# The first weight block of a transformer layer's last projection is split two products before the MLP ends, and the projection's PSUM banks swap parity

## The reference

```python
x = x + mix @ w_out                                   # mix: long convolution and attention
h = _rmsnorm(x, mlp_norm_w) @ w_mlp1
x = x + jnp.square(jax.nn.relu(h)) @ w_mlp2
gate = jax.nn.sigmoid(x @ w_ple_gate)
x = x + gate * _rmsnorm(p_l @ w_ple_proj, ple_norm_w)
```

## Time and profile before

| | |
|---|---|
| median of three runs | 1794.86 us (1792.33, 1794.86, 1794.9) |
| the profiled execution | 1794.4 us, its span 1792.6 us |
| TensorE matmul busy | 1745.6 us, 97% of the span |
| TensorE weight load busy | 1583.3 us, 88% |
| VectorE busy | 1332.4 us, 74% |
| ScalarE busy | 728.3 us, 41% |
| GpSimd busy | 408.2 us, 23% |
| mean granted TensorE clock | 0.993 of full speed |

### The profile page before, as it was taken

The page is one execution under the profiler, slowest core; times in us unless marked ns, Lnnn a source line. Parts: engine busy times, 40 slices in busy tenths (PEclk is TensorE's granted clock), DMA queues, the critical chain, the costliest instruction groups (busy, mean ns, idle before and its releaser), DMA issues.

```text
span 1792.6 us, 26437 instructions
## 1 busy us (share of the span) xinstructions
PE 1745.6 (97%) x10563; PEld 1583.3 (88%) x10563; DVE 1332.4 (74%) x1671; ACT 728.3 (41%) x1149; POOL 408.2 (23%) x256
## 2 busy tenths in 40 slices
PE   8999999999999999999999999999899999999999
PEld 5566788888899987888999999999899999998887
DVE  4695376887999988579765555557999898996634
ACT  6112311246777778146333333334233333333511
POOL 0000000003222220001222222124848373840000
PEclk9999999999999999999999999999999999999999
DMA  9223145132110013423232222328241413102121
GB/s 361 87 77 129 65 172 178 62 147 79 51 42 21 16 60 117 146 104 131 76 130 99 99 94 100 105 77 320 83 175 31 170 42 141 42 1 77 36 93 60
DMA packets 59058, 183.65 MB, mean 102 GB/s; under 512 B 6901, under 2 KB 7669, under 8 KB 58424
## 3 DMA queue, kind: packets, MB, share of 16 engines
q1 hardware_dynamic: 58936, 181.96, 28.6%
HBM read 138.58 MB, written 43.35 MB: 101 GB/s over the span
## 4 chain that ended last, share of the span: by engine, by line
PE 81%; DVE 11%; ACT 3%; issue 2%; DMA 2%; SPq 1%; POOL 0%; DVEq 0%; ACTq 0%; POOLq 0%
PE ps L3247 40%; PE ps L2724 21%; PE ps L3107 3%; PE ps L3135 3%; PE ps L3119 2%; PE ps L2783 2%; PE ps L2810 2%; PE ps L2822 2%; DVE K L1655 1%; PE ps L3016 1%; DVE ptl L2299 1%; PE ps L2771 1%; DVE gmax L2252 1%; DMA wst<-wb 1%; DVE cv L1655 1%
## 5 line engine op out<-in xcount | busy, mean ns | idle before, releaser
L3247 PE MATMUL ps<-rV,ringh 128*128 128x320 f32 x1248 | 235.8, 311 | 9.0 <-issue 7.0
L3247 PE MATMUL ps<-rU,ringh 128*128 128x320 f32 x1088 | 204.3, 310 | 3.3 <-issue 2.1
L3247 PEld LDWEIGHTS ps<-rV,ringh 128*128 128x128 f32 x1248 | 197.1, 189 | 10.7 <-issue 8.2
L2724 PE MATMUL ps<-XL,wh 128*128 128x512 f32 x708 | 179.0, 361 | 0.0
L3247 PEld LDWEIGHTS ps<-rU,ringh 128*128 128x128 f32 x1088 | 170.5, 188 | 4.8 <-issue 3.4
L2480 DVE TENSOR_TENSOR fH<-ps,fH 128x640 f32<-128x640 f32 x112 | 90.7, 822 | 112.1 <-PE ps L3247 112.0
L2724 PE MATMUL ps<-XH,wh 128*128 128x512 f32 (+1 forms) x612 | 164.6, 378 | 6.5 <-DVE wl L1632 2.8
L2724 PE MATMUL ps<-XH,wl 128*128 128x512 f32 (+1 forms) x612 | 154.4, 361 | 0.0
L3247 PE MATMUL ps<-rV,ringl 128*128 128x320 f32 x624 | 142.7, 310 | 0.0
L2724 PEld LDWEIGHTS ps<-XH,wh 128*128 128x128 f32 x612 | 105.0, 191 | 40.0 <-issue 18.7
L3247 PE MATMUL ps<-rH,ringh 128*128 128x320 f32 x736 | 137.9, 309 | 1.3 <-DVE rH L2425 1.3
(11 more groups left out here) (408 smaller groups left out, 3893.3 us busy)
## 6 DMA issues: line engine op xcount, KB each, us to landing
hd<-fH SPq DMA_DIRECT2D x64, 320.0 KB, 2.3
wst<-wb SPq DMA_DIRECT2D x34, 512.0 KB, 3.4
wst<-wm SPq DMA_DIRECT2D x30, 512.0 KB, 3.7
fU<-hd SPq DMA_DIRECT2D x32, 320.0 KB, 4.0
fH<-hd SPq DMA_DIRECT2D x24, 320.0 KB, 3.9
wraw<-wm SPq DMA_DIRECT2D x14, 512.0 KB, 3.7
w2b<-wm SPq DMA_DIRECT2D x12, 512.0 KB, 7.2
xraw<-xT SPq DMA_DIRECT2D x8, 640.0 KB, 10.2
```

Source lines behind the costliest of these rows:

```text
L2724: ins = mm(acc(jslot)[:, o:o + n], sub(a[slot], s), b[:, o:o + n], start=(first and k == 0 and a is wh and b is xh), stop=(last and k == l ...
L3247: ins = mm(out[:, c, :], a[:, w], two(b(xs[kk]))[:, c, :], start=kk == 0 and a is h and b is hi_of, stop=kk == 3 and a is l)
```

## The change

The split of B_PLE moves up on both engines: ScalarE's waits for product 221 in place of 222, and VectorE's stands ahead of the sum of product 223, with a wait for product 221. The sixteen jobs of the projection and the gate take the accumulator of their own parity in place of the other one, and the projection's first two jobs wait for the sums of products 222 and 223, by name. The split of B_PLE+1 stays where it was.

```diff
@@ ScalarE
-            split(B_PLE, (mm_done, product_done(222)))
+            split(B_PLE, (mm_done, product_done(221)))
             split(B_PLE + 1, (mm_done, product_done(223)))
 ...
-                fn((dsq if m else dss)[:, :], acc(J_PLE + m + 1), ACT.Square).then_inc(pp_sq, 1)
+                fn((dsq if m else dss)[:, :], acc(J_PLE + m), ACT.Square).then_inc(pp_sq, 1)
                 act.wait_ge(acc_free, J_PLE - NPROD + m)
-                fn(pp[m], acc(J_PLE + m + 1), ACT.Copy).then_inc(acc_free, 1)
+                fn(pp[m], acc(J_PLE + m), ACT.Copy).then_inc(acc_free, 1)
 ...
-                    fn(dsq[:, :], acc(j + 1), ACT.Sigmoid).then_inc(acc_free, 1)
+                    fn(dsq[:, :], acc(j), ACT.Sigmoid).then_inc(acc_free, 1)
@@ VectorE
+            dve.wait_ge(mm_done, product_done(221))
+            split(B_PLE, B_PLE % 2)
             output_sum(111)
-            dve.wait_ge(mm_done, product_done(222))
-            split(B_PLE, B_PLE % 2)
             dve.wait_ge(mm_done, product_done(223))
             split(B_PLE + 1, (B_PLE + 1) % 2)
@@ TensorE
                 if m % 4 == 0:
                     weights_ready(B_PLE + m // 4)
                 if m < 2:
-                    pe.wait_ge(ps_read, PS_READ + 112 + 110 + 2 * m)
-                linear(J_PLE + m, J_PLE + m + 1, (B_PLE + m // 4) % 2, (2 * (m % 4), 2 * (m % 4) + 1),
+                    pe.wait_ge(ps_read, PS_READ + 112 + 111 + m)
+                linear(J_PLE + m, J_PLE + m, (B_PLE + m // 4) % 2, (2 * (m % 4), 2 * (m % 4) + 1),
                        x2[6:8], [(h_lo, 1), (h_lo, 2)])
 ...
-                linear(J_GATE + m, J_GATE + m + 1, (B_GATE + m) % 2, range(KD), x2)
+                linear(J_GATE + m, J_GATE + m, (B_GATE + m) % 2, range(KD), x2)
```

More of the change, by code:

```diff
@@ L1471, in _ @@
                         act.wait_ge(mm_done, j + 1 + c)
-                        fn(dsq[:, o:o + n], acc(j + 1)[:, o:o + n], ACT.Sigmoid).then_inc(acc_free, 1)
+                        fn(dsq[:, o:o + n], acc(j)[:, o:o + n], ACT.Sigmoid).then_inc(acc_free, 1)
                 if m < 6:
@@ L3285, in _ @@
                 weights_ready(B_GATE + m)
-                linear(J_GATE + m, J_GATE + m + 1, (B_GATE + m) % 2, range(KD), x2,
+                linear(J_GATE + m, J_GATE + m, (B_GATE + m) % 2, range(KD), x2,
                        [(n_lo, KD + 28 + 112 + 1 + k) for k in range(KD)] if m == 0 else (),
@@ L3290, in _ @@
                 weights_ready(B_GATE + m)
-                linear(J_GATE + m, J_GATE + m + 1, (B_GATE + m) % 2, range(KD), x2)
+                linear(J_GATE + m, J_GATE + m, (B_GATE + m) % 2, range(KD), x2)
             weights_ready(B_GATE + 6)
-            linear(J_GATE + 6, J_GATE + 7, B_GATE % 2, range(KD), x2)
+            linear(J_GATE + 6, J_GATE + 6, B_GATE % 2, range(KD), x2)
             weights_ready(B_GATE + 7)
@@ L3297, in _ @@
             for o, n in TOKENS:
-                ins = passes(acc(J_GATE + 8)[:, o:o + n],
+                ins = passes(acc(J_GATE + 7)[:, o:o + n],
                              [((sub(wh[last], k), sub(wl[last], k)), (x2[k][0][:, o:o + n], x2[k][1][:, o:o + n]))
```

## The result

| | before | changed |
|---|---|---|
| median of ten runs | 1792.74 us | 1788.36 us |
| lowest to highest | 1790.85 to 1794.9 | 1787.3 to 1791.08 |
| the profiled execution (its span) | 1794.4 (1792.6) | 1789.74 (1788.0) |

The ratio is 0.9979, 95% interval 0.9971 to 0.9987: about 3.8 us (2.3 to 5.2). So the changed kernel is faster, though the interval doesn't say that it is by over 0.2%; the two medians alone differ by 4.4 us. The forecast was a gain of 3.65 us, 0.203%. But its time, 1791.2, stands 2.8 us above the measured median, and its range of 1789.6 to 1793.4 misses it. The gain was right within what the runs can tell, and the base it was taken from was not: the median of before's first three runs, 1794.86, was 2.1 us above that of ten.

What follows compares the result with a forecast made beforehand. TensorE was taken as the bound (busy 97% of the span). Pause 2.05 plus clock fall 1.60 gave 3.65 us, other edits 0: 1794.86 - 3.65 = 1791.2 us, range 1789.6 to 1793.4.

Steps and rivals of the forecast that it cites:

- The base: Before's time from which the gain was subtracted: 1794.86 us, the median of three runs.
- one more fall in luck: Low end of the range: one further clock fall of 1.6 us missing from the whole run, giving 1789.6 us.
- The pause: TensorE's idle time between the MLP's last product and the last (PLE) projection, all removed: 2.05 us.
- the seam's unknown: Remainder where the projection's first matmul follows the last product without a wait: within 0.3 us either side, taken as 0.
- The clock fall: Projection's first nine matmuls, slow behind the pause, run at full clock: 3.37 us becomes 1.77, saving 1.60.
- half the gain: Rival: the pause goes but no clock fall is saved, or the side sums get one; 1792.8 us, chance 0.25.
- The edits at nothing: ScalarE's earlier split, VectorE's reordered split, the swapped banks, and the second block with its load: each priced at 0.
- The slack of the split: VectorE's early split of B_PLE ends at about 1639.0, before the sum of product 223 at 1640.49: 1.5 us.
- nothing waits at the side sums: Answers the slower rival: late projection additions make TensorE wait at the side sums, with a fall; 1796.5 us, chance 0.04.
- rival of an unfinished split: VectorE's split not over when product 223 ends, so part of the pause stays; 1791.9 to 1794.2 us, chance 0.08.

Runs made afterwards that it cites:

- f3: The kernel before, unchanged, measured against itself: 0.9999 of before, runs from 1790.8 to 1795.23 us.
- e1: The changed kernel with ScalarE's copy of the first weight block waiting for product 222 again: 0.9977 of before, median 1789.06 us.
- e3: The kernel before with only the bank parity and its waits changed, both splits left where they were: 1.0002 of before.
- e2: The kernel before with both splits of the first block early, old bank parity, job 0 waiting for the sum of product 223: 0.9992 of before, median 1790.54 us.
- f1: The kernel before with TensorE's pause ahead of the last projection filled by twelve matmuls whose result is thrown away: 0.9999 of before.
- g1: The kernel before with the pause filled by twelve thrown away matmuls, the same kernel as f1 once more: 0.9999 of before.
- g3: The changed kernel with the side sums and the broadcast one step later: 0.9988 of before, median 1790.94 us.
- h1: The kernel before with the pause filled by thrown away matmuls and the side sums' one-column matmuls in two halves: 0.9989 of before.
- h2: The kernel before with three runs of twenty one-column matmuls in halves (near 220 and 343 us, and the side sums): 0.9999 of before, runs 1791.87 to 1793.22 us.

## Why the prediction was right or wrong

**The base: the step that failed.** "1794.86 - 3.65 = 1791.2" took the median of three as the kernel's time, where ten runs gave 1792.74. Over 126 runs before's mean is 1792.8 with a standard deviation of 1.2, and the profiled execution (clock 0.993) was of the quarter with the lowest clock, with falls near 222 and 345. Both come and go: 5 and 6 of the 14 profiles with undivided sums there have them. With the better base of 1792.74 the same sum gives 1789.1, 0.7 above the median measured, and the same range 1787.5 to 1791.3, which holds it.

**The range: too narrow on the low side.** It allowed "one more fall in luck". The prediction had the evidence for more in hand: three runs 2.6 us apart, and a fall at 219.53 named as uncertain. It used them for the seam's fall and the side sums', but not for the base.

**The pause and the seam: right, the remainder a little off.** All 2.05 us of idle time went. The first matmul came 2.21 us earlier behind the last product's last group (2.50 to 0.29), so the seam's unknown, bounded by 0.3 us and taken as 0, was 0.16 in the change's favour.

**The clock fall: right in kind and in size.** The term was 1.60, and the nine matmuls now take 1.62 us less; behind them nothing more was gained (33.46 against 33.47 us up to the side sums). The prediction also held it possible that some runs of before escaped this fall, and put 0.25 on half the gain. In the five profiles with a pause of 2 us or more at the seam it was never missing; what differs from run to run is other falls. The Trainium skill (TensorE: Matmul & The Clock Gate, "What's actually happening") says that slow matmuls differ in number from run to run of one kernel, and the traces agree (before's first profile has seven falls, f3's six); the step from that to this place was mine. The time lost to the clock fell by 1.5 us, close to a whole fall.

**The edits at nothing: right.** ScalarE's Copy (e1), the parity by itself (e3), the load and the second block cost nothing. The slack of the split was 1.56 us, forecast 1.5. The additions ended at 1669.31 + 1.49 = 1670.8, 3.86 ahead of the side sums at 1674.66, where before had 3.87: they moved up with TensorE. That job 0 under the old parity "could not have used the earlier split" was too strong: e2 used it for 1.09 of the 2.05 us.

**The rivals.** No pause was left and nothing waits at the side sums, so those two fall. Two figures of the rival of an unfinished split didn't follow from its own working. A block landing at 1637 leaves no pause: the Copy and the split would end near 1639.3, ahead of product 223, and e1, whose Copy started as late as before's, had none. And its upper end of 1794.2 is 0.7 above the 0.7 us of pause and a fall of 1.6 that it names (1793.5). The rival of half the gain named the side sums as a place that could take the fall. It did not in any profile of the changed kernel, but in e2, f1, g1 and g3 it did. As g3's 1.5 us suggest, the changed kernel owes a part of its gain to where its side sums stand, which the prediction had only as a chance: that part is luck.

## What to carry to other kernels

When an engine idles for a result while later work is queued behind that wait, look whether the later work could run first, and whether the buffers it frees are those that the next stage writes: here the banks alone gave nothing, the order alone about half of the pause, and both together some 3.8 us. Price a pause of TensorE with the fall of the clock that the trace shows behind it, and look where the next fall could come once it is gone. Before giving an absolute time, ask how many falls the profiled run has that another run may not have, and set the range by that.

## What the runs showed of the hardware

A fall of TensorE's clock to 1.2 GHz costs 1.7 us in this kernel each time (0.66 of full speed over 5 us). At the seam it stood behind a pause of 2.05 us in four profiles of four and behind 3.18 us in the one that has it, and not behind 0.96 us in one. Elsewhere a pause of 1.13 us had one behind it and one of 1.45 us, 7 us later in the same profile (e1), had none. Behind twenty one-column matmuls in a row, through which the profile counts TensorE as busy, one stands in some profiles: in 5 and 6 of 14 near 222 and 345 us, and in 4 of 13 behind the side sums. In two halves with 1.8 us of wide matmuls between they had none (three profiles with divided side sums, two with the other two divided); so few could be chance, and h1's ratio and h2's spread are the better evidence. A fall avoided at one place can turn up at another: filling the pause gave 0.9999 while the side sums stood undivided and 0.9989 when they were divided, and with them one step of 1.76 us later the changed kernel gave 0.9988 beside 0.9980 in the same group (intervals that overlap, means 1.6 us apart). Why just these places fall in one kernel and not in the other was not shown here.
